# Weight tiles split anew in every unit, in place, and the blocks' round trip through DRAM issued by ScalarE

## What is computed

```python
h = jnp.einsum('btd,dc->btc', x, w_in)
ya = _deltanet_group(qa, ka, va, za, ba, aa, conv_w, a_log, dt_bias, norm_w)
yb = _swa_group(qb, kb, vb, zb, sinks)
y = jnp.einsum('btc,cd->btd', jnp.concatenate([ya, yb], axis=-1), w_out)
return _layernorm(DEEPNORM_ALPHA * x + y, ln_g, ln_b)
...
a_mat = jnp.where(strict, jnp.einsum('bhncd,bhnsd->bhncs', k_beta, k) * decay, 0.0)
t_mat = lax.linalg.triangular_solve(eye + a_mat, jnp.broadcast_to(eye, a_mat.shape), ...)
```

## Time and profile before

| | before |
|---|---|
| median of three runs | 1250.78 us |
| the profiled execution | 1249.48 us |
| its span, first to last instruction | 1247.7 us |
| mean granted TensorE clock | 0.970 |
| TensorE busy | 1149.6 us (92%) |
| VectorE busy | 650.1 us (52%) |
| ScalarE busy | 505.5 us (41%) |
| GpSimd busy | 198.0 us (16%) |

### The profile page before, as it was taken

One profiled execution on the slowest core, in us unless ns is written; L12 is line 12 of the kernel. 1 busy time (PEld: TensorE's weight loads), 2 busy tenths in 40 slices (PEclk: granted clock), 3 DMA queues, 4 the chain that ended last, 5 costly groups with the idle time before them and its releaser, 6 DMA issues. The chain is left out here.

```text
span 1247.7 us, 19748 instructions
## 1 busy us (share of the span) xinstructions
PE 1149.6 (92%) x7340; PEld 900.9 (72%) x7340; DVE 650.1 (52%) x1996; ACT 505.5 (41%) x1475; POOL 198.0 (16%) x268
## 2 busy tenths in 40 slices
PE   4988989888999999999999999999899989899997
PEld 2766767666777868786786878777686868687776
DVE  3345554645355464646356364745437363636565
ACT  3363636363352625353352433336233534353220
POOL 4522323122210101023000101012100000000340
PEclk9998989898999999999999999999999999999999
DMA  6753745545572543632436362625244343522232
GB/s 212 287 191 123 252 164 161 179 136 153 161 237 102 164 160 104 211 127 78 150 132 193 124 192 79 201 84 172 85 165 157 110 137 110 168 79 61 94 109 84
DMA packets 63887, 183.57 MB, mean 147 GB/s; under 512 B 16240, under 2 KB 28976, under 8 KB 50480
## 3 DMA queue, kind: packets, MB, share of 16 engines
q1 hardware_dynamic: 63792, 182.32, 44.1%
HBM read 138.22 MB, written 44.07 MB: 146 GB/s over the span
## 5 line engine op out<-in xcount | busy, mean ns | idle before, releaser
L760 PE MATMUL bank<-xr,w 128*128 128x512 f32 x2496 | 684.8, 414 | 5.1 <-ACT conv_in L1091 3.2
L760 PEld LDWEIGHTS bank<-xr,w 128*128 128x128 f32 x2496 | 455.5, 193 | 108.5 <-issue 14.8
L733 POOL TENSOR_TENSOR x_tile<-x_tile,gain 128x256 f32<-128x256 f32 x40 | 28.1, 736 | 716.6 <-DVE x_tile L1484 716.6
L810 PE MATMUL bank<-wo,y_split 128*128 128x512 f32 x432 | 118.8, 409 | 0.0
L810 PEld LDWEIGHTS bank<-wo,y_split 128*128 128x128 f32 x432 | 76.2, 188 | 17.1 <-issue 1.9
L1410 DVE SCALAR_TENSOR_TENSOR kq<-conv_in,convw_all,kq 128x512 f32<-128x512 f32 x96 | 76.5, 796 | 3.4
L1332 ACT ACTIVATE blocks<-bank 128x128 f32<-128x128 f32 x64 | 17.8, 277 | 149.0 <-PE bank L1027 148.8
L1605 DVE TENSOR_TENSOR y_step<-blocks,y_cols 128x60 f32<-128x60 f32 (+14 forms) x240 | 49.7, 207 | 49.7 <-DMA blocks<-n_spill 42.0
L1227 ACT ACTIVATE score<-score,neg_max 128x256 f32<-128x256 f32 (+1 forms) x128 | 62.5, 490 | 16.8 <-DVE neg_max L1572 16.8
L1297 ACT ACTIVATE blocks<-bank 128x256 f32<-128x256 f32 (+1 forms) x64 | 24.4, 382 | 105.1 <-PE bank L974 73.7
L1692 DVE SCALAR_TENSOR_TENSOR t<-bank,cols_all,v_tok 128x128 f32<-128x128 f32 x64 | 22.3, 348 | 84.8 <-PE bank L1012 84.8
(11 more groups left out here) (214 smaller groups left out, 1762.1 us busy)
## 6 DMA issues: line engine op xcount, KB each, us to landing
w<-w_split SPq DMA_DIRECT2D x78, 1024.0 KB, 5.0
w_split<-w SPq DMA_DIRECT2D x26, 1024.0 KB, 4.9
blocks<-n_spill SPq DMA_DIRECT2D x16, 512.0 KB
y_spill<-y_out SPq DMA_DIRECT2D x30, 256.0 KB, 6.3
y_tile<-w_in SPq DMA_DIRECT2D x13, 512.0 KB, 6.1
x_tile<-w_in SPq DMA_DIRECT2D x13, 512.0 KB, 6.2
y_tile<-y_spill SPq DMA_DIRECT2D x12, 512.0 KB, 6.7
x_tile<-x SPq DMA_DIRECT2D x12, 512.0 KB, 5.6
```

Of the source, the lines that this page charges most:

```text
L733: nc.gpsimd.tensor_tensor(res[:, part], res[:, part], gain[:, part], ALU.mult).then_inc(scaled.sem, 1)
L760: ins = nc.tensor.matmul(bank[at % 2][:], w[:, turn % 3, wp, k, :], xr[:, xp, k], start=(step == 0), stop=(step == 3 * KT - 1))
L810: ins = nc.tensor.matmul(bank[at % 2][:], y_place(t)[:, yp, k], wo[:, k, wp, half * UNIT:(half + 1) * UNIT], start=(step == 0), stop=(step ...
```

## The change

It has these parts.

- `w_split` and its stores and loads are gone. Each of the 104 tile uses loads the raw tile (512 KB) into the low part's place of a ring of four (`wl`, seen as float32 in `wl_raw`), ScalarE writes the high part to a ring of three (`wh`), and GpSimd subtracts in place. The split that belongs to the last job of a slot is held back and stands behind the blocks' store of the next opening (`split_weight`).
- `w_out` is split in s1 and s2 instead of s3, in place too; so are y and, from the third unit on, half of x.
- VectorE picks the diagonal blocks out of `n_t` (a product with a mask and a sum, `picked`), ScalarE stores them with one DMA and issues their load.
- In an opening VectorE does the pick, the low parts of x and the maxima ahead of `kq` and `pt`, not behind them.
- `TAIL = 0`: gain and shift of the LayerNorm go from GpSimd to VectorE for the first twelve token tiles too, and `norm_wait` says when.
- `Places`, `AT_VTOK` and the order of jobs change a little; `o_scaled` has a buffer of its own.

```diff
-TILES_W = 26
-TAIL = 12
+HIGHS, LOWS = 3, 4
+TAIL = 0
...
-        return ["q", "k", "v", "z", "o0", "o1", "bz", "bq"]
+        return ["q", "k", "v", "z"] + (["o0", "o1", "bz"] if i == AH - 2 else ["o0", "bz", "o1"]) + ["bq"]
...
-AT_SCORES0, AT_VTOK, AT_TURNS0, AT_VALUES0 = 0.09, 0.13, 0.24, 0.31
+AT_SCORES0, AT_VTOK, AT_TURNS0, AT_VALUES0 = 0.09, 0.16, 0.24, 0.31
...
-        first = 0.47 if short else 0.36 if long else 0.42
+        first = 0.49 if short else 0.375 if long else 0.44
...
+            def load_w(turn):
+
                 if turn < len(W_JOBS):
...
+                    if turn >= LOWS:
+                        sp.wait_ge(dense_done, W_JOBS[turn - LOWS] + 1)
+                    sp.dma_start(wl_raw[:, turn % LOWS].rearrange("p k n -> p (k n)"), w_in[w_tile(JOBS[W_JOBS[turn]])])\
+                        .then_inc(raw_in[turn % LOWS], 16)
...
             def w_hi(turn):
...
+                act.wait_ge(raw_in[turn % LOWS], 16 * (turn // LOWS + 1))
+                if turn >= HIGHS:
+                    act.wait_ge(dense_done, W_JOBS[turn - HIGHS] + 1)
+                nc.scalar.activation(wh[:, turn % HIGHS], wl_raw[:, turn % LOWS], ACT.Copy).then_inc(w_high, 1)
...
+                if at + 1 < len(JOBS) and JOBS[at + 1].n > job.n >= 0:
+                    held.extend(split)
+                else:
+                    for part, which in split:
+                        part(which)
...
+            def store_blocks(n):
+                after(act, picked, n, 2)
+                act.dma_start(n_spill[n], y_step[:].rearrange("p t c -> p (t c)")).then_inc(n_stored.sem, 16)
+
+            def load_blocks(n):
+                after(act, n_stored, n, 16)
...
+                store_blocks(n)
+                split_weight()
                 after(act, small, n, 3)
...
+                load_blocks(n)
                 after_jobs(n, 0.12)
                 weights(n, 0)
...
+            def norm_wait(t):
+
+                return 0.325 if t < 8 and t % CH < CH - 2 else 0.1
...
+                nc.vector.tensor_tensor(pt[:].rearrange("p t (b c) -> p t b c", c=BASE),
+                                        n_t[:].rearrange("p t (b c) -> p t b c", c=BASE),
+                                        own_block[:].unsqueeze(1).unsqueeze(3).to_broadcast(wide), ALU.mult)\
+                    .then_inc(picked.sem, 1)
+                after(dve, picked, n, 1)
+                nc.vector.tensor_reduce(y_step[:], pt[:].rearrange("p t (b c) -> p t c b", c=BASE), AXIS.X, ALU.add)\
+                    .then_inc(picked.sem, 1)
```

More of the change, by code:

```diff
@@ L1 @@
+import math
 from contextlib import ExitStack
@@ L112, in w_tile @@
             "kb": 16, "vb": 17, "bq": 18 + 2 * i, "bz": 19 + 2 * i}[job.kind]
-W_FIRST = {w_tile(JOBS[at]): turn for turn, at in enumerate(W_JOBS[:TILES_W])}
-def w_landings(turn):
-    return sum(1 for t in range(TILES_W, turn + 1) if t % 3 == turn % 3)
+WO_JOBS = ("k", "v", "z", "bq")
 def slot_span(n):
@@ L345, in build_layer @@
         ea_ready = sem("ea_ready")
-        x_in = [sem(f"x_in{i}") for i in range(5)]
+        x_in = [sem(f"x_in{i}") for i in range(4)]
         x_high = counter("x_high", 4)
@@ L603, in _ @@
             load_x(0, 3)
-            load_raw(0)
-            load_raw(1)
+            for turn in range(LOWS):
+                load_w(turn)
             for dst, source in ((ident[:], c_ident), (convw_all[:], conv_w), (dtb[:], dt_bias), (alog[:], a_log),
@@ L609, in _ @@
                 sp.dma_start(dst, source).then_inc(const_in, 16)
-            for turn in range(2):
-                store_w(turn)
-            after_jobs(-1, 0.6)
+            after_jobs(-1, 0.65)
             load_decay(0)
@@ L662, in _ @@
                 after_jobs(n, 0.3)
+                if t is not None and 0 < i < AH - 1:
+                    store_tile(t - 1)
                 if t is not None and i < AH - 1:
@@ L667, in _ @@
                     load_x_tile(8)
+                if n < 2:
+                    for k in range(4 * n, 4 * n + 4):
+                        load_wo(k)
                 after_jobs(n, 0.55)
@@ L681, in _ @@
                     load_decay(n + 1)
-                if t is not None and i < AH - 1:
+                if t is not None and i == AH - 2:
                     store_tile(t)
@@ L1110, in _, with split_weight @@
             place = [0]
+            held = []
+            def split_weight():
+                for part, which in held:
+                    part(which)
+                held.clear()
             def after_job(at):
@@ L1291, in slot @@
                 t = out_tile(n)
-                if t is not None and i < AH - 1:
-                    round_y(t)
                 def take(dst, b, k):
@@ L1301, in slot @@
                 take(t0[:], half_tiles(bank[5]), 1)
+                if t is not None and i < AH - 1:
+                    round_y(t)
                 after_jobs(n, at.t16)
@@ L1328, in slot @@
                             round_y(15)
-                        silu(n, True)
+                        if not (n < SLOTS - 1 and t is None or i < AH - 2):
+                            silu(n, True)
                     after_jobs(n, at.chunk(c, 2 / 3))
```

330 lines of the change are left out of this document (141 added, 189 removed).

## The result

The changed kernel takes **1300.8 us** (median of 4 runs, 1299.5 to 1303.5), the kernel before 1248.0 us beside it: a ratio of 1.043 (95% interval 1.040 to 1.046). The profiled execution went from 1247.7 to 1299.9 us of span, 52 us longer; the forecast's sum was +32.

The account below looks back on a forecast made before the run. TensorE, busy 92% of the span, was taken as the bound, through its own work and its waits. Slot terms 8 + 2 - 4 + 7 + 18 + 1 = +32 us on 1249.5 led to 1282 us, range 1236 to 1306.

Parts of the forecast that it names:

- GpSimd's company: GpSimd slowing VectorE's base inverse steps: 1.9 us a tile, in every slot but s15, eating gains from earlier landing or later places.
- The signs: Profile marks named beforehand: TensorE waits, clock and busy times that would show the forecast, and findings that would make it wrong.
- Blocks, 4.6 us behind `n_t`: Openings: pick, store issue, split, scaling and load issue put the blocks' load 4.6 us behind n_t, against 4.7 before.
- No gain in where the base inverse starts: Openings: blocks may land 1 to 2 us sooner, but VectorE is still at its convolution; no gain except in s0.
- s7 and s11, +18: Unit turns: no slack at the quotient, so +5.7 us at L881, +1.3 at L963, +2 of clock; 9 us each.
- s5, s6, s9 and s10, +7: Gain and shift delay the quotient and, in s6 and s10, the chunk chain; a wait for t goes: +7 us.
- s12 to s14, +8: Longer waits for k_dec +5.4 us, base inverse giving back 2.7, lost clock +5.1: +8 us.
- s0 to s3, +2: w_out splits add +2 us each in s1 and s2, s0 -3, s3 +1 from later x: +2 us.
- s4 and s8, -4: Waits at the base inverse fall from 2.8 to about 2.2 us, short enough for a full clock: -4 us.
- rival 3: ScalarE waits for raw tiles, 78 more splits at 0.5 us each, 40 us: 1320 us; chance 0.08.
- Rival 1: The base inverse waits at L963 go: 30 us and about 15 of clock, some 1205 us; half gives 1227; chance 0.18.

Follow-up runs that it names:

- a_xlate: The changed kernel, but SyncE issues the last two x parts in s7 and s11 only once the blocks have landed; 1292.9 us, ratio 1.038.
- a_poolwait: The changed kernel, but GpSimd starts low parts that fell into the base inverse or divide(n, 0) only once those are done; 1261.0 us, ratio 1.013.
- b_pick_act: The kernel before with only the blocks' new way: pick on VectorE, one store and one load issued by ScalarE; 1268.8 us, ratio 1.019.
- b_pick_sp: The kernel before with only the blocks' new way, but SyncE issues the one store and one load; 1231.1 us, ratio 0.989.
- a_splitlate: The changed kernel, but the held weight split stands behind ScalarE's k_dec scaling and the blocks' load; 1313.1 us, ratio 1.055.

## Why the prediction was right, and where it wasn't

The direction held, and so did the mechanism of the forecast in its outline, that the opening costs more than the blocks give back. But a loss of the same size was another: keeping GpSimd out of two stretches of VectorE's work gave 37 us back (some 12 of them were lost in the kernel before as well), and the forecast had let GpSimd's company cancel against gains. The blocks' own way is a gain once SyncE issues it (0.989). The time was 1282 by the forecast and 1300.8 by the clock; the sum was 20 us short of the profiled 52. Step by step:

- **The signs.** One sign by which the forecast was to be wrong did come: TensorE has no wait at the `turns` of s7 or s11, where about 5 us each were forecast. The others didn't: in s5 the load comes 4.5 us behind `n_t`, not under 4, and VectorE idles for blocks no more, but the waits at the base inverse are 34.8 us (some 30 forecast). ScalarE's 578 us and GpSimd's 362 (590 and 380) and a clock of 0.964 (under 0.97) fit; a wait for `k_dec` of about 1 us in s4 did not show.
- **Blocks, 4.6 us behind `n_t`.** In s5 the load is issued at 434.05, 4.5 us behind the end of `n_t` (429.51). The pick takes 0.69 + 1.01 = 1.7 us (1.5 taken). "No gain in where the base inverse starts" came true: 21.3 us into s5 now, 20.0 before, though no longer for the blocks' sake: VectorE's own work ahead of it, gain and shift among it, now ends last.
- **s7 and s11, +18.** The total is right (+19.7), its place isn't. The wait was put at `turns` (L881) behind the quotient. It stands at L777, one link earlier in the same chain: the copy of `za` that I had delayed with the rest also frees TensorE's bank. I had taken it for late work of ScalarE's, not as a releaser of TensorE. I also missed the store's 6.2 us behind 1 MB of x: of the 8.5 us about 3.5 are that (a_xlate). The waits at the base inverse shrank there (2.4 us before, 1.5 and 1.9 after), where I gave 1.3 more each, and s7 ran at a clock of 0.93 and not 0.98, 5 us over its length where I gave 2. So that the size came out is in part luck.
- **s5, s6, s9 and s10, +7.** This term was mis-sized most: +16.1. The price of a tile beside the inverse was right: 3.9 us for two tiles in s5, against 1.9 for one. The count was wrong. I took one tile into the inverse, cancelled against later places, and none beside the quotient; the timeline shows two and one. The second costs 1.9 us; the third 1.7, of which 1.15 are the quotient's and 0.5 those of the small sum ahead of it (L1567, 0.69 and not 0.16 us). That is 3.6 us in each slot, 14 over four. a_poolwait takes it out: s5 goes from 71.5 to 68.2 us and the four from 287.5 to 273.4. What is then left over the kernel before is 1.9 us, so gain and shift, from which the +7 was worked out, seem to cost less than I gave them.
- **s12 to s14, +8.** Measured +2.1. The waits for `k_dec` came (2.2, 2.8 and 2.8 us), and of the 5.1 us of clock some 3: it was granted at 0.95, 0.97 and 0.94 after against 0.97 in all three before. s1's clock was too low a bound for a slot with two waits; why s1 ran lower than these no run here says. What I had too small is what comes back: the waits at the base inverse fell from 10.3 to 6.2 us in the three slots (2.7 given), and those of 0.8 us at `turns` in s13 and s14 went.
- **s0 to s3, +2**, measured +8.0. Most of what is missing is s3, +4.2 where I gave +1: its wait for the low part of x grew from 2.7 to 7.5 us, and only 3.1 us of that came back at the base inverse (3.7 to 0.6). x stands behind the load on ScalarE there too: that wait is 8.3 us in b_pick_act and 3.2 in b_pick_sp.
- **s4 and s8, -4**, measured +2.3. The wait at the inverse went, but another came: ScalarE waits for a raw tile (2.45 us in s4, 3.28 in s8), copies the scores late, and TensorE waits 2.5 and 3.3 us at L862. The clock, from which most of the -4 was to come, stayed at 0.98. This is rival 3, small: 10.0 us of ScalarE in 4 waits, and not 40.
- **Rival 1** (the waits at L963 go) had its first half, no waiting for blocks, and not its second. Its condition that the issues on ScalarE cost nothing failed: b_pick_sp, where they are on SyncE, is faster than before.

The Trainium skill's page "DMA: Bandwidth & Descriptors" (Issuing engines are not separate DMA queues) says that DMAs of several issuers interleave on the same 16 engines and that another issuer saves only the sequencer's time. b_pick_act agrees: a load issued 1.1 us sooner arrived 1.9 us later. I had read it as "no gain"; the runs show a loss of 14 us or more, because the move also changed what SyncE issues next.

The Trainium skill's page "SBUF — State Buffer" (Who interferes with whom) has VectorE, with two SBUF inputs, and GpSimd exclude each other for a whole instruction. The steps of s5 agree better than I had granted: while GpSimd is at it, one step ends per piece of GpSimd's (2.81 / 4 = 0.70 us), and its price is that less the step's own 0.2.

## What to carry to other kernels

When a helper engine gets more work, count, slot by slot, where each of its instructions will fall beside the engine that the bound waits for; the price per overlap is easily read, and the count decides the sum. A few waits that move the helper's work off that stretch were worth 3% here. When a DMA's issue moves to another queue, ask what the old queue issues in its place, and what stands on the new one behind the wait for its data.

## What the runs showed of the hardware

- A store of 32 KB, issued on its own queue 0.9 us behind 1 MB of another, took 6.2 us to land against 1.4 in the median slot, and at most 3.2 in a_xlate, where x comes later. A queue of its own was no way past the other's transfers.
- VectorE's `TENSOR_SCALAR` on one SBUF tile (the quotient) is slowed beside GpSimd as well: 2.29 us for four in s5, 2.76 in a_splitlate, 1.14 without company.
- GpSimd loses too beside large instructions: its four pieces take 2.8 us beside small steps and 4.33 us beside the convolution (3 instructions of 512 elements, 3.38 us and not 2.32).
